# Weights in split float32: three slots instead of two, the rest written over the loaded words

## The reference, cut to what matters

```python
h = rmsnorm(x, norm1_g[l]);  u = h @ w_in[l]
mix = concat(mlstm(u...), diff_attention(u...), hgrn2(u...))
x = x + mix @ w_out[l]
x = x + relu(rmsnorm(x, norm2_g[l]) @ w_up[l])**2 @ w_down[l]
```

```python
h = h + 0.5 * rms_norm(swiglu(rms_norm(h, g0), gate, up, down), g1)      # a, c
h = h + rms_norm(pool_mixer(rms_norm(h, g2)) or dilated_mixer(...), g3)
h = h + 0.5 * rms_norm(swiglu(rms_norm(h, g4), gate, up, down), g5)      # b, d
```

## Time and profile before

| what | value |
|---|---|
| median of 3 runs | 3792.15 us (3792.1 to 3793.68) |
| the profiled execution, its time | 3790.01 us |
| its span, first to last instruction | 3788.7 us |
| mean granted clock of TensorE | 0.934 of full |
| TensorE busy | 3443.1 us, 91% |
| VectorE, ScalarE, GpSimd busy | 36%, 30%, 32% |
| subtractions on GpSimd (L413) | 288, 1209.1 us |
| roundings on ScalarE (L406) | 288, 503.5 us |
| transfers | 296.75 MB, mean 78 GB/s |

### The profile page before, as it was taken

How to read it: one execution, slowest core, us unless ns; L and a number is a source line. 1 busy time by engine, 2 the same in 40 slices (tenths; PEclk the granted TensorE clock), 3 DMA queues, 4 the chain that set the end, 5 groups by cost and what they waited for, 6 DMA issues and landing times.

```text
span 3788.7 us, 36989 instructions
## 1 busy us (share of the span) xinstructions
PE 3443.1 (91%) x15506; PEld 2733.4 (72%) x15506; DVE 1360.0 (36%) x2212; ACT 1133.6 (30%) x1553; POOL 1221.5 (32%) x300
## 2 busy tenths in 40 slices
PE   7887899998976999999997789998999979769998
PEld 5654588886744788888886678886888857547887
DVE  4437531314257421222126541224221253573123
ACT  2234342322134332322222232223222233422222
POOL 4210044443200244434442234443444431014442
PEclk9887799999978899999998899999999989869998
DMA  3110033332200133333332223323433322013332
GB/s 121 60 52 1 12 100 100 93 96 68 78 19 1 56 100 93 96 100 89 101 86 73 86 67 92 108 89 111 125 93 106 84 97 84 1 39 91 98 96 71
DMA packets 462182, 296.75 MB, mean 78 GB/s; under 512 B 14330, under 2 KB 454192, under 8 KB 462016
## 3 DMA queue, kind: packets, MB, share of 16 engines
q1 hardware_dynamic: 453664, 277.09, 25.0%
q10 hardware_dynamic: 8352, 17.30, 1.3%
HBM read 285.97 MB, written 8.39 MB: 78 GB/s over the span
## 4 chain that ended last, share of the span: by engine, by line
PE 82%; DVE 14%; ACT 3%; issue 1%; POOL 0%; SPq 0%; DMA 0%; ACTq 0%; DVEq 0%
PE bank L473 24%; PE bank L474 24%; PE bank L475 24%; PE bank L313 9%; DVE ta L525 1%; DVE x L750 1%; DVE ta L748 1%; DVE ta L1132 1%; DVE xl L773 1%; DVE qkv L1914 0%; DVE u L1428 0%; DVE ta L1911 0%; DVE scr L1669 0%; DVE sqacc L767 0%; DVE tb L1912 0%
## 5 line engine op out<-in xcount | busy, mean ns | idle before, releaser
L413 POOL TENSOR_TENSOR wlo<-raw,whi 128x2048 fp32r<-128x2048 f32 (+3 forms) x288 | 1209.1, 4199 | 2530.0 <-ACT whi L406 2530.0
L473 PE MATMUL bank<-xh,whi 128*128 128x512 f32 x2432 | 973.6, 400 | 70.4 <-DVE xl L773 39.4
L474 PE MATMUL bank<-xl,whi 128*128 128x512 f32 x2432 | 960.0, 395 | 0.0
L475 PE MATMUL bank<-xh,wlo 128*128 128x512 f32 x2432 | 959.3, 394 | 0.0
L406 ACT ACTIVATE whi<-raw 128x2048 fp32r<-128x2048 f32 (+3 forms) x288 | 503.5, 1748 | 685.6 <-PE bank L475 650.7
L473 PEld LDWEIGHTS bank<-xh,whi 128*128 128x128 f32 x2432 | 465.1, 191 | 187.1 <-POOL wlo L413 33.2
L475 PEld LDWEIGHTS bank<-xh,wlo 128*128 128x128 f32 x2432 | 464.4, 191 | 99.2
L474 PEld LDWEIGHTS bank<-xl,whi 128*128 128x128 f32 x2432 | 465.6, 191 | 93.8
L473 PE MATMUL bank<-ah,whi 128*128 128x512 f32 x1216 | 473.0, 389 | 0.0
L474 PE MATMUL bank<-al,whi 128*128 128x512 f32 x1216 | 473.0, 389 | 0.0
L475 PE MATMUL bank<-ah,wlo 128*128 128x512 f32 x1216 | 473.0, 389 | 0.0
(11 more groups left out here) (333 smaller groups left out, 3046.1 us busy)
## 6 DMA issues: line engine op xcount, KB each, us to landing
raw<-in_ffn_w_gate SPq DMA_DIRECT2D x88, 512.0 KB, 4.0
raw<-in_ffn_w_up SPq DMA_DIRECT2D x88, 512.0 KB, 5.2
raw<-in_w_up SPq DMA_DIRECT2D x64, 512.0 KB, 4.7
raw<-in_w_down SPq DMA_DIRECT2D x64, 512.0 KB, 5.2
raw<-in_w_in SPq DMA_DIRECT2D x56, 512.0 KB, 4.7
raw<-in_ffn_w_down SPq DMA_DIRECT2D x64, 384.0 KB, 4.1
raw<-in_ffn_w_down SPq DMA_DIRECT2D x64, 320.0 KB, 3.7
raw<-in_w_out SPq DMA_DIRECT2D x16, 512.0 KB, 4.4
```

Source lines behind the costliest of these rows:

```text
L413: g.e.tensor_tensor(self.wlo[slot][:, 0:n], self.raw[slot][:, 0:n], self.whi[slot][:, 0:n].bitcast(F32), ALU.subtract).then_inc(self.lo_ma ...
L473: pe.e.matmul(bank, hi[:, at:at + P], xh, start=k == ks[0], stop=False)
L474: pe.e.matmul(bank, hi[:, at:at + P], xl, start=False, stop=False)
L475: last = pe.e.matmul(bank, lo[:, at:at + P], xh, start=False, stop=k == ks[-1])
```

## The change

There are three slots. `wlo` is given the same addresses as `raw`: GpSimd writes the rest over the loaded words. `whi` has three slots of its own, so the memory is as large as before. A slot of `raw` can now be loaded only when TensorE is done with unit u-3, and `sp_load` waits for that. `act_hi(u)` waits for the same event and for the landing. ScalarE rounds and GpSimd subtracts two units ahead: `act_dense` calls `act_hi(u + 2)` in the middle of the steps of unit u, for the gates (one step) ahead of it; the extra call in phases with a norm is gone; at the start `act_hi(1)` and `pool_lo(1)` come ahead of the first x and the sums of squares. `pool_lo` of the third unit of a phase with a norm waits until VectorE has made that norm's diagonal and copy, an event ticked at the end of `dve_norm`'s call. For the gates only the words that were loaded are rounded and subtracted. PSUM banks still alternate by the parity of the unit.

```diff
-        self.raw = [at(f"raw{s}", [P, SLOT], F32, offset=RING_AT + s * SLOT * 4) for s in range(2)]
-        self.whi = [at(f"whi{s}", [P, SLOT], F32R, offset=RING_AT + (2 + s) * SLOT * 4) for s in range(2)]
-        self.wlo = [at(f"wlo{s}", [P, SLOT], F32R, offset=RING_AT + (4 + s) * SLOT * 4) for s in range(2)]
+        self.raw = [at(f"raw{s}", [P, SLOT], F32, offset=RING_AT + s * SLOT * 4) for s in range(3)]
+        self.wlo = [at(f"wlo{s}", [P, SLOT], F32R, offset=RING_AT + s * SLOT * 4) for s in range(3)]
+        self.whi = [at(f"whi{s}", [P, SLOT], F32R, offset=RING_AT + (3 + s) * SLOT * 4) for s in range(3)]
...
     def sp_load(self, u):
-        if u >= 2:
-            sp.wait_ge(self.lo_made, self.lo_made[u - 2])
+        if u >= 3:
+            sp.wait_ge(self.tile_done, self.tile_done[u - 3])
...
+    def loaded(self, u):
+        ph, ring = UNITS[u], [t[u % 3] for t in (self.raw, self.whi, self.wlo)]
+        if ph.tiles:
+            return [t[:, 0:words(ph)] for t in ring]
+        return [t[:, 0:KC * HD].rearrange("p (k s n) -> p k s n", s=2, n=32)[:, :, :, 0:4] for t in ring]
+
     def act_hi(self, u):
-        if u >= len(UNITS) or u <= self.rounded:
+        if u >= len(UNITS):
             return
-        self.rounded = u
-        a, slot, n = self.a, u % 2, words(UNITS[u])
+        a, slot = self.a, u % 3
+        if u >= 3:
+            a.wait_ge(self.tile_done, self.tile_done[u - 3])
         a.wait_ge(self.raw_landed[slot], self.raw_landed[slot][u])
-        if u >= 2:
-            a.wait_ge(self.tile_done, self.tile_done[u - 2])
-        a.e.activation(self.whi[slot][:, 0:n], self.raw[slot][:, 0:n], ACT.Copy).then_inc(self.hi_made.tick(u), 1)
+        raw, hi, lo = self.loaded(u)
+        a.e.activation(hi, raw, ACT.Copy).then_inc(self.hi_made.tick(u), 1)
 
     def pool_lo(self, u):
         g.wait_ge(self.hi_made, self.hi_made[u])
-        g.e.tensor_tensor(self.wlo[slot][:, 0:n], self.raw[slot][:, 0:n], self.whi[slot][:, 0:n].bitcast(F32),
-                          ALU.subtract).then_inc(self.lo_made.tick(u), 1)
+        if ph.norm and u == ph.first + 2:
+            g.wait_ge(self.norm_v, self.norm_v["diagonal of", ph.name])
+        raw, hi, lo = self.loaded(u)
+        g.e.tensor_tensor(lo, raw, hi.bitcast(F32), ALU.subtract).then_inc(self.lo_made.tick(u), 1)
...
     def dve_dense(self, name):
             if j == 0 and ph.norm:
                 self.dve_norm()
+                self.norm_v.tick("diagonal of", name, by=0)
...
     def act_dense(self, name):
-            self.act_hi(u + 1)
-            for _ in range(ph.nk * ph.tiles if ph.tiles else 1):
+            steps = ph.nk * ph.tiles if ph.tiles else 1
+            for n in range(steps):
+                if n == steps // 2:
+                    self.act_hi(u + 2)
                 yield
             if j == 0 and ph.norm:
                 self.act_norm()
-
-                self.act_hi(u + 2)
...
     def act_start(self):
         self.act_hi(0)
+        self.act_hi(1)
...
     def gpsimd(self):
         self.pool_lo(0)
+        self.pool_lo(1)
         self.pool_start()
         for ph in PHASES.values():
             for j in range(ph.count):
-                self.pool_lo(ph.first + j + 1)
+                self.pool_lo(ph.first + j + 2)
```

More of the change, by code:

```diff
@@ L271, in __init__ @@
         self.x_landed, self.parameters = self.new_signal("x_landed"), self.new_signal("parameters_landed")
-        self.raw_landed = [self.new_signal("raw_landed0"), self.new_signal("raw_landed1")]
+        self.raw_landed = [self.new_signal(f"raw_landed{s}") for s in range(3)]
         self.hi_made, self.lo_made = self.new_signal("hi_made"), self.new_signal("lo_made")
@@ L375, in sp_load @@
     def sp_load(self, u):
-        sp, ph, slot = self.sp, UNITS[u], u % 2
-        j, raw = u - ph.first, self.raw[u % 2]
-        if u >= 2:
-            sp.wait_ge(self.lo_made, self.lo_made[u - 2])
+        sp, ph, slot = self.sp, UNITS[u], u % 3
+        j, raw = u - ph.first, self.raw[slot]
+        if u >= 3:
+            sp.wait_ge(self.tile_done, self.tile_done[u - 3])
         if ph.tiles == 0:
@@ L410, in pool_lo @@
             return
-        g, slot, n = self.g, u % 2, words(UNITS[u])
+        g, ph = self.g, UNITS[u]
         g.wait_ge(self.hi_made, self.hi_made[u])
-        g.e.tensor_tensor(self.wlo[slot][:, 0:n], self.raw[slot][:, 0:n], self.whi[slot][:, 0:n].bitcast(F32),
-                          ALU.subtract).then_inc(self.lo_made.tick(u), 1)
+        if ph.norm and u == ph.first + 2:
+            g.wait_ge(self.norm_v, self.norm_v["diagonal of", ph.name])
+        raw, hi, lo = self.loaded(u)
+        g.e.tensor_tensor(lo, raw, hi.bitcast(F32), ALU.subtract).then_inc(self.lo_made.tick(u), 1)
     def pe_operand(self, name, j, k):
@@ L440, in pe_dense @@
         for j in range(ph.count):
-            u, slot = ph.first + j, (ph.first + j) % 2
+            u, slot, banks = ph.first + j, (ph.first + j) % 3, 2 * ((ph.first + j) % 2)
             pe.wait_ge(self.lo_made, self.lo_made[u])
@@ L453, in pe_dense @@
             if ph.tiles == 0:
-                bank = self.bank[2 * slot]
+                bank = self.bank[banks]
                 for k in range(KC):
@@ L470, in pe_dense @@
                 at = k * w + t * P
-                bank = self.bank[2 * slot + t][:]
+                bank = self.bank[banks + t][:]
                 xh, xl = self.operand(name, j, k)
@@ L2264, in build @@
                 self.unit = self.norms = self.cleared = 0
-                self.rounded = -1
                 program()
```

## The result

| kernel | median, us | runs | span of the profiled execution |
|---|---|---|---|
| before | 3791.46 | 9 | 3788.7 |
| changed | 3804.41 | 9 | 3802.8 |

A forecast was written before the change was run, and what follows sets the result against it. The prediction took TensorE, busy 91% of the span, as the bound, with VectorE operations held by GpSimd subtractions deciding. Its eight parts summed to +5.7 us on the median 3792.15, so 3797.9; 8 in 10 need 3779 to 3809.

The forecast's parts named there:

- my likeliest case: Whole kernel: gains and new collisions nearly cancel, +5.7 us, 3797.9 us, no change that counts; chance 0.62.
- Part 3: Units 1 behind b, k and d, and one wait in o: TensorE's stalls for wlo go, -17.7 us.
- Part 4: Pooling: VectorE gets unit 0 earlier, new blocks included, first pool_out unit done earlier, -7.2 us (bounds -11 and -2).
- Part 6: Head of the mixers, both layers: subtractions hold VectorE and a rounding delays ScalarE, +3.1 and +2.5 us.
- Part 7: Tail of mLSTM, both layers: the subtraction of in_ah's last slot holds L1164, +3.7 us each, +7.4.
- Part 5: q phase: earlier start by 5.8 us, against subtractions on the chain of L1911 and L1914, together +0.9 us.
- Part 8: Start: first L868 held up to 4.6 us, unit 1's stall goes; from -5.7 to +5, middle +0.5 us.
- Part 1: Behind the last unit of back phases a, b, c: a subtraction holds the last L627, +3.4 us each, +10.2.
- Part 2: Behind pool_out and o: subtractions hold L627, behind o a rounding also precedes the squares; +2.0 and +4.0 us.
- The statement: VectorE operations that read a PSUM bank pass while GpSimd subtracts, cited from L616; no size given.
- ScalarE brakes the mixers: Rival: in the mixers act_hi's wait for a load stops ScalarE, each of 26 woven units loses 1 us, 3824; chance 0.12.
- It doesn't do what it says: Rival: the stalls for wlo stay, since the load also starts later; 3792 us, chance 0.06.

The follow-up runs named there:

- old-places run: Changed kernel with the roundings at the start, in the mixers and in q put back where the kernel before had them: 3783.5 us, ratio 0.9977.
- quarters run: Changed kernel with each GpSimd subtraction of a unit issued as four of a quarter of the words: 3772.5 us, ratio 0.9950 to the kernel before.
- e3: Changed kernel without the wait of the third unit's subtraction for the norm's diagonal: 3811.2 us, one run.
- e6: Changed kernel with roundings at the old places (start, mixers, q) and subtractions in quarters: 3770.1 us, ratio 0.9938 to the kernel before.
- e9: Kernel with old places and quarters, with the rounding in o moved before the last of eight steps instead of the fifth: 3766.8 us.

## Why the prediction was right or wrong

The range held the time (3804.4 in 3779 to 3809) and the mechanism was the forecast one, part by part, but my likeliest case said "no change" and it is slower: 6.5 us above the forecast by the medians, 8.4 above the sum in the account (14.1 for 5.7).

- **Right.** Parts 3, 4, 6 and 7 are within 0.9 us each. The operations named as victims were the victims, and steady units moved by 0.0. In the pooling, too, it was as worked out: both big subtractions of pool_out hold an L611 (L622 after, 4.61 and 4.66 us). The old-places run shows parts 5, 6, 7 and half of 8 as causes, the quarters run parts 1 and 2.
- **Luck.** The mixers between tail and out were put at 0; they moved by +2.4 in layer 0 and -2.2 in layer 1, which cancel by chance.
- **Behind o, +4.0 forecast, +7.3 measured: the largest miss.** I saw both pieces, the rounding ahead of the squares and the second held L627, but priced them together at about one hold.

```profile
3384.16 1.92 ACT L413 ACTIVATE whi<-raw 128x2048 fp32r<-128x2048 f32 x1 [2.26 <-DMA raw<-in_ffn_w_up]
...
3385.98 0.61 ACT L742 ACTIVATE tb<-f 128x512 f32<-128x512 f32 x1
...
3386.62 4.64 DVE L638 TENSOR_TENSOR sqacc<-sqacc,tb 128x512 f32<-128x512 f32 x1 [3.40 <-ACT tb L742]
...
3394.40 4.50 POOL L424 TENSOR_TENSOR wlo<-raw,whi 128x2048 fp32r<-128x2048 f32 x1 [3.69 <-ACT whi L413]
...
3394.88 4.57 DVE L638 TENSOR_TENSOR sqacc<-sqacc,tb 128x512 f32<-128x512 f32 x1 [1.03 <-ACT tb L742]
```

  ScalarE stops for the load (2.26) and rounds (1.92) while the square that L638 wants stands behind; the pair of kernels with short subtractions gives 4.1 us for that alone. The holds add the rest.
- **Part 1, +10.2 forecast, +12.3 measured.** The holds were 3.3 each, as said (3.4). I left out what TensorE does after a longer idle time: 0.8 us each at half the clock.
- **Part 5, +0.9 forecast, +3.0 measured.** The hold of the second L1926 came as worked out. L1805 started on the positions 6.65 us after their issue (3115.42 to 3122.07), not 5.2. The earlier trace rows shows 4.7 us of another queue, but 5.2 was right for this very transfer in the kernel before (3105.08 to 3110.23). There the two reloads of q were issued 2.0 and 2.4 us behind it; after, they were issued 1.9 and 1.5 us ahead of it, which the forecast did not move along. That they are the cause is likely, not shown by a run of its own. So unit 1 gave 0.5 instead of 2.2, and the later units cost 4.0 instead of 3.1, less 0.5 at the end of the attention.
- **Part 8.** The forecast was the middle of a range from -5.7 to +5, so +1.3 says little for it. The quarters run leaves +0.8 and the old places +0.7.
- **A row that does not show what it was cited for.** No subtraction runs beside the L616 at 2010.44. The statement holds all the same: the L616 at 2017.24 took 0.69 us inside a subtraction from 2013.68 to 2018.26.
- **The rivals.** "ScalarE brakes the mixers" fell: between head and tail no unit's end moved by more than 0.1 us. But a rounding that holds up ScalarE is real and costs where ScalarE is already late: by its own 1.9 us at the head, by the wait for its load at the tail and behind o. "It doesn't do what it says" fell with the waits for `wlo`.
- **What stays open.** The stretch of the mixers between the tail of mLSTM and the out phase varies from kernel to kernel though its own instructions are the same. In layer 1 the old places with whole and with quartered subtractions give

```profile
1058.00:1255.60 197.60, 134.49 (x669) 79.10 (x669) 125.50 (x293) 85.62 (x171) 0.00 (x0) 0.74 0.03 9
```

  and

```profile
1056.40:1258.50 202.10, 140.59 (x668) 82.15 (x668) 125.59 (x293) 85.62 (x171) 0.00 (x0) 0.70 0.03 9
```

  VectorE and ScalarE do the same, GpSimd nothing; only the granted clock (0.74, 0.70) and so TensorE's busy time differ. The stretch is also most of why `e3` stands 7 us above the changed kernel: 4.1 us in layer 0 (clock 0.72 against 0.75) and 2.5 in layer 1, where the mean clock is no lower (0.76 against 0.75), so the clock does not explain all of it. It is probably behind the spread of 10 us among the runs of `e6` and `e9`, of which only one each was profiled. What sets the clock there was not found; totals of single runs can't be read below some 5 us, the steps of the account can.

## What to carry to other kernels

A transfer or a GpSimd operation that is moved ahead to be "off the path" should be walked to the operation it now lands on: here 25 us won (parts 3 and 4) were outweighed by 39 us of holds on late VectorE operations and of roundings ahead of late ScalarE instructions (the other parts). Cut long GpSimd operations that read SBUF into pieces where VectorE is late and their own end is not awaited; where it is awaited, pieces lengthen it (waits of 42.3 us became 50.6). Put an instruction that waits for a load behind the evacuation that stands next on its engine, not merely late among the steps ahead of it.

## What the runs showed of the hardware

- A VectorE operation with two SBUF operands waits for the whole GpSimd operation in front of it, however small it is: 3.14 us for two words (0.16 by itself). That settles for this kernel the question the prediction had to leave open, in favour of the Trainium skill (SBUF — State Buffer, Who interferes with whom), by which the order of issue decides who waits and the operation's shape does not.
- The hold is mutual and by instruction. Between pieces one VectorE operation gets in: behind b in the quarters run a quarter took 1.72 us after the held L643, and the diagonal's four parts 2.25 us instead of 0.87.
- A piece has a price of its own. A quarter of 512 words takes 1.29 us with no VectorE instruction beside it, and one follows the other every 1.25 us, where a whole subtraction of 2048 words takes 4.6.
- After 5.46 us of idle time TensorE's next eight small matmuls took 1.86 us at a granted clock of 0.50, after 2.17 us only 1.05 at 1.00.
- The same small load landed 5.15 us after its issue in the kernel before, 6.63 in the changed one, 7.53 with the old places and 7.41 in the kernel before without subtractions; in these three, reloads were issued ahead of it.
